# A two-block transformer layer on one core: second half of two gate products by tile, rotary key in other PSUM banks, first turned tiles under the side input's products

## The chip, the cores and the metric

The kernel runs on one core of one Trainium2 chip. The metric is device time in microseconds (us) from one launch to its end, the median over several runs. A profiled execution gives a trace of every instruction. The engines are TensorE (PE), VectorE (DVE), ScalarE (ACT), GpSimd (POOL) and SyncE (SP). Work that PE does is written to PSUM, which has eight banks of 128 partitions by 512 floats.

## The reference

The reference takes 512 tokens of width 1024 through four mixers. The last two are the layers of `second_block`. Each of these ends in a gated side input, and this is what the change touches:

```python
for i in range(DEPTH):
    xn = rmsnorm_2(x, norm_g[i])
    if i % N_MIXERS == 0:
        y = mixer_na(xn, na_w_in[j], na_rpb[j], na_w_out[j])
    else:
        y = mixer_mla(xn, mla_w_in[j], mla_q_norm[j], mla_w_qb[j],
                      mla_kv_norm[j], mla_w_kvb[j], mla_w_out[j])
    h = x + y
    gate = jax.nn.sigmoid(rmsnorm_2(h, ple_norm[i]) @ ple_w_gate[i])
    x = h + gate * (p[i] @ ple_w_proj[i])
return rmsnorm_2(x, final_norm)
```

`mixer_mla` begins with `xn @ w_in`, whose columns are c_q (384), c_kv (256), the rotary key (32) and z (1024). The rotary key is multiplied with cosines and sines.

## The kernel before

Every product in float32 is made of three: high part by low part, low by high, high by high. A weight matrix comes in units of 1 MB (128 x 2048 floats). SP loads a unit into `w_raw` (L308), ACT writes its rounded high part `w_hi` (L339, `split_high`), POOL writes the rest `w_lo` (L348, `split_low`) and counts up `w_ready`. There are three slots of such units. SP loads unit n once PE has signalled that the unit before it in the slot is used up (`consumed`): `w_used` for the first unit of a pair, `bank_done` for the second.

Activations are four tiles of 128 tokens. To be multiplied, a tile of x is squared and summed on ACT (`square_x`, L658), POOL makes the reciprocal root (`root_x`, L704 and L706), DVE scales it (`norm_tile`, L746), PE transposes it with 8 transposes into two of the banks 4 to 7 (`turn_tile`, L623), ACT copies it to `u_hi` (`high_tile`, L664) and DVE writes the rest to `u_lo` (`low_tile`, L752). Each step waits for the one before it by a semaphore (`chain_x_square`, `chain_x_rstd`, `chain_normed`, `chain_turned`, `chain_high`, `chain_low`).

The order on each engine is written out by hand in one function for each engine and stage. The stages that matter, in order, twice (layer 0 with `na_out` and `ple0`, layer 1 with `mla_out` and `ple1`):

- `na_out` or `mla_out`, a product of 1024 to 1024 in two halves of 512 columns (i = 0, 1). Each half has two weight units (a = 0, 1) and four tiles (j), with all tiles of unit a = 0 before those of a = 1. DVE adds it to x (L591).
- `ple_tensor`: the side input's product, two halves of four tiles of 6 matmuls each. Between them PE turns the four tiles of the normalised residual.
- `gate_tensor`: the gate's product, again two halves with two units each, which are called g0, g1 (i = 0) and g2, g3 (i = 1) below. One (a, j) is 12 matmuls. ACT takes a finished bank through the sigmoid (`take`, L1778), DVE multiplies it with the side input (L1815) and adds it to x (L1818).
- In layer 0, `mla_cq` (units cq0, cq1, 384 columns) and `mla_ckv` (ckv0, ckv1, 256 columns) follow, then `mla_rope` (one unit, 48 matmuls of 512 columns) and `mla_z`. In `mla_cq` PE turns the rest of the next chain's tiles: `project_turning` takes rows of (a, j, tile to turn in the middle). Layer 1 ends with the last norm and the store of the output by SP (L328).

The first entries in the list that sets where tiles are turned in `mla_cq` and the function that takes the rotary key read:

```python
INTERLEAVED = ((0, 0, 1), (0, 1, 2), (1, 0, 3), (0, 2, None), ...
project_tensor(pe, "mla_rope", banks=2)          # banks 0 and 1
project_tensor(pe, "mla_z", only=(0,))           # banks 0 to 3
```

`wait_bank` lets PE write a bank when both takers' counts (`bank_free`) have passed it, so `mla_z` in bank 0 waits for DVE's product with the cosines (L1942).

Of the kernel before, what the change touches and what calls it, by code (L numbers as in the profile page):

```python
# [24 lines left out]
NT = T // P  # L25
# [74 lines left out]
def _program(nc, A, out):  # L100
    with ExitStack() as ctx:
# [523 lines left out]
                tr.then_inc(chain_turned, 1)  # L625

        HALF_BY_HALF = ((0, 0, 2), (0, 1, 3), (0, 2, None), (0, 3, None), (1, 0, None), (1, 1, None), (1, 2, None), (1, 3, None))
        INTERLEAVED = ((0, 0, 1), (0, 1, 2), (1, 0, 3), (0, 2, None), (0, 3, None), (1, 1, None), (1, 2, None), (1, 3, None))

        def project_turning(pe, c, name, order):  # L630

            run = RUNS[name]
            for a, j, turning in order:
                pe.wait_ge(w_ready, run["unit"] + a + 1)
                if a == 0:
                    wait_bank(pe, run, 0, j)
                    pe.wait_ge(chain_low, c.two + 2 * (j + 1))
                mm = products(pe, run, 0, a, j, between=None if turning is None else lambda: turn_tile(pe, c, turning))
                if a == 0 and j == 3:
                    mm.then_inc(w_used, 1)  # L640
                if a == 1:
                    mm.then_inc(bank_done, 1)

        def square_y(act, c, name, i, j):
            act.wait_ge(bank_done, 4 * (RUNS[name]["block"] + i) + j + 1)
# [1030 lines left out]
        def ple_tensor(pe, c, nth):  # L1676

            run = RUNS[f"ple{nth}_proj"]
            pe.wait_ge(p_lo, nth + 1)
            turning = {(0, 0): 1, (0, 2): 2, (1, 0): 3}  # L1680
            for i in range(2):
                pe.wait_ge(w_ready, run["unit"] + 1)
                for j in range(NT):
                    wait_bank(pe, run, i, j)
                    products(pe, run, i, 0, j).then_inc(bank_done, 1)
                    if (i, j) in turning:
                        turn_tile(pe, c, turning[i, j])
# [77 lines left out]
        def gate_tensor(pe, c, name, chain):  # L1765
            pe.wait_ge(chain_low, c.two + 2 * NT)
            project_tensor(pe, name, only=(0,))
            project_tensor(pe, name, only=(1,), between=chain and {(1, 1, 3): lambda: turn_tile(pe, chain, 0)})

        def gate_scalar(act, c, nth):  # L1770

            name = f"ple{nth}_gate"
            run = RUNS[name]

            def take(i, j):
                act.wait_ge(bank_done, 4 * (run["block"] + i) + j + 1)
                act.wait_ge(e_used, 8 * nth + 4 * i + j + 1)
                nc.scalar.activation(at(SIG + j * 512), bank(j), ACT.Sigmoid).then_inc(bank_free["act"], 1)  # L1778

            split_next(act, name, 0, 0)  # L1780
            for j in range(NT):
                take(0, j)
            split_next(act, name, 0, 1)
            if c is final_chain:
                take(1, 0)
                take(1, 1)
                square_x(act, c, 0)
                take(1, 2)
                square_x(act, c, 1)
                take(1, 3)  # L1790
                square_x(act, c, 2)
                square_x(act, c, 3)
                return
            split_next(act, name, 1, 0)
            take(1, 0)
            take(1, 1)
            square_x(act, c, 0)
            take(1, 2)
            square_x(act, c, 1)
            high_tile(act, c, 0)  # L1800
            take(1, 3)
            split_next(act, name, 1, 1)
            square_x(act, c, 2)
            high_tile(act, c, 1)
            square_x(act, c, 3)
            high_tile(act, c, 2)
            high_tile(act, c, 3)

        def gate_vector(dve, c, nth):
# [11 lines left out]
                take(0, j)  # L1821
            wait_gain(dve, c.pre)
            take(1, 0)
            take(1, 1)
            norm_tile(dve, c, 0)
            take(1, 2)
            if c is final_chain:
                norm_tile(dve, c, 1)
                take(1, 3)
                norm_tile(dve, c, 2)  # L1830
                norm_tile(dve, c, 3)
                return
            low_tile(dve, c, 0)
            norm_tile(dve, c, 1)
            take(1, 3)
            low_tile(dve, c, 1)
            norm_tile(dve, c, 2)
            norm_tile(dve, c, 3)
            low_tile(dve, c, 2)
            low_tile(dve, c, 3)  # L1840

        def gate_pool(pool, c, nth):

            n = RUNS[f"ple{nth}_gate"]["unit"] + 2
            split_low(pool, n)
            split_low(pool, n + 1)
            if c is final_chain:
                for t in range(NT):
                    root_x(pool, c, t)
                return  # L1850
            for part in range(4):
                split_low(pool, n + 2, part)
            root_x(pool, c, 0)
            root_x(pool, c, 1)
            split_low(pool, n + 3, 0)
            split_low(pool, n + 3, 1)
            root_x(pool, c, 2)
            root_x(pool, c, 3)
            split_low(pool, n + 3, 2)
            split_low(pool, n + 3, 3)  # L1860


        COS, SIN = gain[0][:, 0:T], gain[0][:, T:2 * T]
# [71 lines left out]

        def mla_rope_vector(dve):

            dve.wait_ge(rope_in, 16)

            def take(i, j):  # L1940
                if j == 0:
                    return nc.vector.tensor_tensor(at(ROPE_TMP), bank(0), COS, ALU.mult)  # L1942
                return nc.vector.tensor_tensor(at(QT), bank(1), SIN, ALU.mult)
            project_vector(dve, "mla_rope", take, banks=2)
            run = RUNS["mla_rope"]
            dve.wait_ge(bank_free["dve"], 4 + run["taken"] + 4)
            done("dve", nc.vector.tensor_tensor(at(QT), at(QT), at(ROPE_TMP), ALU.add))
            settle("dve", dve)
            nc.vector.tensor_scalar(k_rope[0], at(QT), 1.0, None, ALU.mult).then_inc(rope_high, 1)
# [51 lines left out]
        def _(pe):  # L2001
# [28 lines left out]
            for name in ("na_z", "na_q"):  # L2030
# [3 lines left out]
            begin(pe, na_flow)  # L2034
            pair_tensor(pe, na_flow)
            project_tensor(pe, "na_out", gated_by=na_flow, only=(0,), begun=True)
            project_tensor(pe, "na_out", gated_by=na_flow, only=(1,),
                           between={(1, 1, 3): lambda: turn_tile(pe, ple_chains[0], 0)})
            ple_tensor(pe, ple_chains[0], 0)
            gate_tensor(pe, ple_chains[0], "ple0_gate", mla_chain)  # L2040
            project_turning(pe, mla_chain, "mla_cq", INTERLEAVED)
            project_tensor(pe, "mla_ckv")
            project_tensor(pe, "mla_rope", banks=2)
            project_tensor(pe, "mla_z", only=(0,))
            project_tensor(pe, "mla_z", only=(1,), between={(1, 1, j): (lambda j: lambda: latent_turn(pe, j))(j) for j in range(NT)})
            pe.wait_ge(lat_low, 2 * NT)
            for name in ("mla_k", "mla_v", "mla_q"):
# [4 lines left out]
            project_tensor(pe, "mla_out", gated_by=mla_flow, only=(1,),  # L2052
                           between={(1, 1, 3): lambda: turn_tile(pe, ple_chains[1], 0)})
            ple_tensor(pe, ple_chains[1], 1)
            gate_tensor(pe, ple_chains[1], "ple1_gate", None)

# [314 lines left out]
```

## Time and profile before

| | us |
|---|---|
| median of 3 runs | 1464.06 (1461.59 to 1464.49) |
| profiled execution | 1463.27 |
| its span in the trace | 1461.5 |
| PE busy | 1373.1 (94%) |
| ACT, DVE, POOL busy | 716.3, 621.6, 780.9 |
| granted PE clock, mean | 0.985 |

The profiled execution took 1.8 us more than its span: what lies around the trace. PE is busy for most of the span, so that time can be found where PE waits. The gate of layer 0 stands in the trace at about 1036 to 1080 us, `mla_cq` to `mla_rope` at 1081 to 1130, the gate of layer 1 at 1408 to 1451, and the last norm behind it.

### The profile page before, as it was taken

The numbers are of one execution on the slowest core, as the hardware profiler recorded it, in microseconds if no ns is written. First come the engines' busy times: TensorE is split into PE (matmuls) and PEld (weight loads), VectorE is DVE, ScalarE is ACT, GpSimd is POOL, SyncE is SP. The second block draws the span as 40 slices with busy tenths as digits, with TensorE's granted clock in tenths as the row PEclk, the third lists the DMA queues.
The fourth block names the chain that finished last, engine by engine and source line by source line (L and its number), as shares of the span: only waits on it lengthen the run. The fifth ranks groups of instructions, "written<-read, shape, count | busy, mean of one in ns | idle before, by whom it ended". The sixth has DMA issues, their size and how long they took to land.

```text
span 1461.5 us, 20933 instructions
## 1 busy us (share of the span) xinstructions
PE 1373.1 (94%) x7818; PEld 1125.8 (77%) x7818; DVE 621.6 (43%) x1606; ACT 716.3 (49%) x1533; POOL 780.9 (53%) x729
## 2 busy tenths in 40 slices
PE   6999999998989999998999999889999999999997
PEld 5887877777878888776778887678878886778785
DVE  3322178886250011883420013962341145887144
ACT  4244278886342323773423234963443354787252
POOL 5355266666554534474753353886456334566652
PEclk9999999999999999889999999999999999999999
DMA  6233210000443231212343233324225221001521
GB/s 238 88 116 115 92 56 27 31 30 32 156 141 119 87 116 58 73 44 91 140 129 131 87 110 118 120 89 161 101 93 196 98 87 59 1 1 59 187 87 58
DMA packets 27876, 139.57 MB, mean 95 GB/s; under 512 B 3328, under 2 KB 3712, under 8 KB 16128
## 3 DMA queue, kind: packets, MB, share of 16 engines
q1 hardware_dynamic: 14112, 98.57, 18.7%
q10 hardware_dynamic: 13664, 39.66, 7.9%
q8 instruction: 63, 1.03, 0.3%
q14 instruction: 37, 0.30, 0.1%
HBM read 129.83 MB, written 8.39 MB: 95 GB/s over the span
## 4 chain that ended last, share of the span: by engine, by line
PE 71%; POOL 11%; DVE 9%; ACT 5%; issue 2%; DMA 1%; ACTq 0%; POOLq 0%; SPq 0%; DVEq 0%
PE psum L393 57%; POOL w_lo L348 3%; POOL w_free L1342 3%; PE psum L1183 3%; PE psum L1164 2%; PE psum L1136 2%; DVE w_free L1232 2%; PE psum L877 2%; DVE u_lo L1245 2%; POOL split L1359 1%; ACT w_hi L339 1%; DVE arena L746 1%; ACT u_hi L1285 1%; PE psum L1149 1%; POOL split L1355 1%
## 5 line engine op out<-in xcount | busy, mean ns | idle before, releaser
L348 POOL TENSOR_TENSOR w_lo<-w_raw,w_hi 128x2048 fp32r<-128x2048 f32 (+2 forms) x118 | 427.0, 3632 | 431.8 <-ACT w_hi L339 431.0
L393 PE MATMUL psum<-u_lo,w_hi 128*128 128x512 f32 (+1 forms) x712 | 279.8, 393 | 0.9 <-DVE arena L1942 0.9
L393 PE MATMUL psum<-u_hi,w_lo 128*128 128x512 f32 (+1 forms) x712 | 277.3, 389 | 0.0
L393 PE MATMUL psum<-u_hi,w_hi 128*128 128x512 f32 (+1 forms) x712 | 277.3, 389 | 0.0
L339 ACT ACTIVATE w_hi<-w_raw 128x2048 fp32r<-128x2048 f32 (+1 forms) x93 | 172.9, 1859 | 155.0 <-DMA w_raw<-in_weights 101.8
L393 PE MATMUL psum<-w_hi,split 128*128 128x512 f32 x608 | 195.7, 394 | 6.0 <-POOL w_lo L348 4.3
L794 ACT ACTIVATE w_free<-w_free,neg_max 128x256 f32<-128x256 f32 (+3 forms) x320 | 183.6, 580 | 12.5 <-DVE neg_max L916 7.4
L393 PEld LDWEIGHTS psum<-u_lo,w_hi 128*128 128x128 f32 (+1 forms) x712 | 133.2, 187 | 30.3 <-POOL w_lo L348 1.3
L393 PEld LDWEIGHTS psum<-u_hi,w_hi 128*128 128x128 f32 (+1 forms) x712 | 133.2, 187 | 28.8
L393 PEld LDWEIGHTS psum<-u_hi,w_lo 128*128 128x128 f32 (+1 forms) x712 | 133.2, 187 | 27.3
L393 PE MATMUL psum<-w_hi,u_lo 128*128 128x512 f32 (+2 forms) x352 | 135.8, 386 | 10.0 <-DVE u_lo L752 7.6
L1245 DVE TENSOR_TENSOR u_lo<-psum,u_hi 128x512 fp32r<-128x512 f32 (+3 forms) x256 | 124.5, 519 | 35.3 <-ACT u_hi L1285 32.3
L393 PEld LDWEIGHTS psum<-w_hi,split 128*128 128x128 f32 x608 | 114.2, 188 | 32.0 <-POOL w_lo L348 6.3
L1285 ACT ACTIVATE u_hi<-psum 128x512 fp32r<-128x512 f32 (+3 forms) x256 | 108.8, 463 | 51.9 <-PE psum L1164 48.1
L393 PE MATMUL psum<-w_hi,u_hi 128*128 128x512 f32 (+2 forms) x352 | 133.4, 379 | 0.0
L393 PE MATMUL psum<-w_lo,u_hi 128*128 128x512 f32 (+2 forms) x352 | 133.3, 379 | 0.0
L1164 PE MATMUL psum<-ident,w_free 128*128 128x128 f32 x704 | 110.6, 283 | 23.4 <-POOL w_free L1342 16.9
L393 PE MATMUL psum<-w_lo,split 128*128 128x512 f32 x304 | 118.4, 390 | 0.0
L1164 PEld LDWEIGHTS psum<-ident,w_free 128*128 128x128 f32 x704 | 77.1, 141 | 48.8 <-POOL w_free L1342 27.8
L1342 POOL TENSOR_SCALAR w_free<-w_free,inv 128x256 f32<-128x256 f32 (+1 forms) x128 | 73.6, 590 | 65.5 <-DVE inv L1238 65.3
L1183 PE MATMUL psum<-u_lo,split 128*128 128x256 f32 (+1 forms) x416 | 102.9, 284 | 0.0
L510 DVE SCALAR_TENSOR_TENSOR split<-psum,split 128x512 fp32r<-128x512 f32 x40 | 27.6, 692 | 171.2 <-ACT split L502 157.2
(193 smaller groups left out, 2194.0 us busy)
## 6 DMA issues: line engine op xcount, KB each, us to landing
w_raw<-in_weights SPq DMA_DIRECT2D x90, 1024.0 KB, 4.8
x<-x_scratch ACTq DMA_DIRECT2D x12, 512.0 KB, 6.7
gain<-in_gains ACTq DMA_DIRECT2D x10, 512.0 KB, 4.6
gain<-in_strips ACTq DMA_DIRECT2D x16, 256.0 KB, 2.9
spare<-in_strips ACTq DMA_DIRECT2D x16, 256.0 KB, 2.9
x_scratch<-x ACTq DMA_DIRECT2D x16, 256.0 KB, 4.2
gain<-in_near ACTq DMA_DIRECT2D x8, 512.0 KB, 4.5
w_raw<-in_near ACTq DMA_DIRECT2D x8, 512.0 KB, 3.7
```

The costliest lines, as they stand in the source:

```text
L339: high = nc.scalar.activation(w_hi[b][:, c], w_raw[b][:, c], ACT.Copy)
L348: low = nc.gpsimd.tensor_tensor(w_lo[b][:, c], w_raw[b][:, c], w_hi[b][:, c].bitcast(F32), ALU.subtract)
L393: mm = nc.tensor.matmul(dst, lhs, rhs, start=(a == 0 and k == 0 and (wl, ul) == (0, 1)), stop=(a + 1 == u and k + 1 == nk and (wl, ul) == ...
L794: nc.scalar.activation(p_map(f, i, m, n), p_map(f, i, m, n), ACT.Exp, scale=-1.0, bias=stat_of(neg_max, i, m), accum_out=stat_of(row_sum, ...
L877: mm = nc.tensor.matmul(head_bank(d, r), buf[:, pt:pt + P], split[:, a + v:a + v + P], start=(kt == 0 and nth == 0), stop=(kt == kts[-1] a ...
L1136: mm = nc.tensor.matmul(score_place(f, i, m), *products[m][nth], start=(nth == 0), stop=(nth == 2 and f is not mla_flow))
L1164: tr = nc.tensor.transpose(psum[:, 4 + m, kt * P:(kt + 1) * P], p_map(f, i, m, n)[:, kt * P:(kt + 1) * P], ident[:])
L1183: mm = nc.tensor.matmul(dst, value_place(f, d, m, kt), pt_pair(buf, d, m, a, b), start=(br == 0 and m == 0 and kt == order[0] and nth == 0 ...
L1232: nc.vector.tensor_tensor_reduce(out=p_map(f, i, m, n), in0=score_bank(i, m, n), in1=bias_of(f, i, m), scale=-1.0, scalar=BIG, op0=ALU.add ...
L1245: nc.vector.tensor_tensor(u_lo[:, c], bank(4 + m, n), u_hi[:, c].bitcast(F32), ALU.subtract).then_inc(f.low, 1)
L1285: nc.scalar.activation(u_hi[:, pt_cols(i, m, n)], bank(4 + m, n), ACT.Copy).then_inc(f.high, 1)
L1342: nc.gpsimd.tensor_scalar(p_map(f, i, m, n), p_map(f, i, m, n), stat_of(inv, i, m), factor_of(f, i, m), ALU.mult, ALU.mult).then_inc(f.p, 1)
```

## The change

There are four edits, and no arithmetic changes.

1. The second half of both gates goes through a new function `project_by_tile`: for each tile both units (a = 0, then 1), so that one tile is complete before the next begins. In layer 0, tiles 0 and 1 of the next chain are turned in the middle of (a, j) = (0, 2) and (0, 3) of it. Before, all four tiles of a = 0 came first, and tile 0 was turned in the middle of (1, 3).
2. ACT, DVE and POOL follow in that order: each take of a tile is followed by that tile's square, root and norm. ACT splits g3 behind the first take of the first half rather than behind the fourth. POOL splits cq0 in two pairs of quarters, each behind a wait for a norm, and cq1 whole behind the last root.
3. `mla_cq` uses `TWO_TO_TURN`: tiles 2 and 3 are turned in the middle of (0, 0) and (0, 2), and all of a = 0 stands before a = 1. The rotary key's product goes to banks 4 and 5, and DVE counts its four banks as free ahead of time.
4. In both layers tile 0 of the chain for the gate is turned behind the first tile of the side input's product, not in the middle of the last tile of `na_out`/`mla_out`; tiles 1, 2, 3 are turned behind (0, 1), (0, 3) and (1, 1), not (0, 0), (0, 2) and (1, 0).

```diff
+        TWO_TO_TURN = ((0, 0, 2), (0, 1, None), (0, 2, 3), (0, 3, None), (1, 0, None), (1, 1, None), (1, 2, None), (1, 3, None))
...
+        def project_by_tile(pe, name, gated_by, between):
+
+            run = RUNS[name]
+            for j in range(NT):
+                for a in range(2):
+                    pe.wait_ge(w_ready, run["unit"] + 2 + a + 1)
+                    if a == 0:
+                        wait_bank(pe, run, 1, j)
+                    mm = products(pe, run, 1, a, j, gated_by=gated_by, between=between.get((a, j)))
+                    if a == 0 and j == 3:
+                        mm.then_inc(w_used, 1)
+                mm.then_inc(bank_done, 1)
...
-            turning = {(0, 0): 1, (0, 2): 2, (1, 0): 3}
+            turning = {(0, 0): 0, (0, 1): 1, (0, 3): 2, (1, 1): 3}
...
-            project_tensor(pe, name, only=(1,), between=chain and {(1, 1, 3): lambda: turn_tile(pe, chain, 0)})
+            project_by_tile(pe, name, None, {(0, 2): lambda: turn_tile(pe, chain, 0), (0, 3): lambda: turn_tile(pe, chain, 1)} if chain else {})
...
             if c is final_chain:
-                take(1, 0)
-                take(1, 1)
                 square_x(act, c, 0)
-                take(1, 2)
-                square_x(act, c, 1)
-                take(1, 3)
-                square_x(act, c, 2)
-                square_x(act, c, 3)
+                for j in range(1, NT):
+                    take(1, j)
+                    square_x(act, c, j)
                 return
...
             take(1, 0)
-            take(1, 1)
             norm_tile(dve, c, 0)
...
+            for j in range(1, NT):
+                take(1, j)
+                if c is not final_chain:
+                    low_tile(dve, c, j - 1)
+                norm_tile(dve, c, j)
+            if c is not final_chain:
+                low_tile(dve, c, 3)
...
         def mla_rope_vector(dve):
 
+            dve.wait_ge(bank_free["dve"], 4 + RUNS["mla_rope"]["taken"])
+            dve.sem_inc(bank_free["dve"], 4)
             dve.wait_ge(rope_in, 16)
...
+            dve.wait_ge(bank_done, 4 * RUNS["mla_rope"]["block"] + 4)
+            done("dve", nc.vector.tensor_tensor(at(ROPE_TMP), bank(4), COS, ALU.mult))
+            done("dve", nc.vector.tensor_tensor(at(QT), bank(5), SIN, ALU.mult))
+            settle("dve", dve)
...
-            project_tensor(pe, "na_out", gated_by=na_flow, only=(1,),
-                           between={(1, 1, 3): lambda: turn_tile(pe, ple_chains[0], 0)})
+            project_tensor(pe, "na_out", gated_by=na_flow, only=(1,))
...
-            project_turning(pe, mla_chain, "mla_cq", INTERLEAVED)
+            project_turning(pe, mla_chain, "mla_cq", TWO_TO_TURN)
             project_tensor(pe, "mla_ckv")
-            project_tensor(pe, "mla_rope", banks=2)
+            project_tensor(pe, "mla_rope", banks=2, base=4)
```

The order of instructions shows this at three places. The first is PE in the second half of layer 0's gate (L393 is a product, L623 the transposes of one tile; slot 0 holds g2, slot 1 holds g3, slot 2 holds cq0). Before, around the turning of tile 0:

```order
L393 MATMUL psum<-w_hi1_52,u_hi_49 128x512
L623 MATMUL psum<-ident,arena_65 128x128 x8
L393 MATMUL psum<-w_hi1_52,u_lo 128x512
L393 MATMUL psum<-w_lo1_55,u_hi_49 128x512
L393 MATMUL psum<-w_hi1_52,u_hi_49 128x512
L393 MATMUL psum<-w_hi1_52,u_lo 128x512
L393 MATMUL psum<-w_lo1_55,u_hi_49 128x512
L393 MATMUL psum<-w_hi1_52,u_hi_49 128x512
L393 MATMUL psum<-w_hi2_53,u_lo 128x384
```

In the changed kernel, around the turning of the same tile, the rows on PE are:

```order
L393 MATMUL psum<-w_hi1_52,u_hi_49 128x512
L393 MATMUL psum<-w_hi0_51,u_lo 128x512
L393 MATMUL psum<-w_lo0_54,u_hi_49 128x512
L393 MATMUL psum<-w_hi0_51,u_hi_49 128x512
L393 MATMUL psum<-w_hi0_51,u_lo 128x512
L393 MATMUL psum<-w_lo0_54,u_hi_49 128x512
L393 MATMUL psum<-w_hi0_51,u_hi_49 128x512
L623 MATMUL psum<-ident,arena_65 128x128 x8
L393 MATMUL psum<-w_hi0_51,u_lo 128x512
```

Tile 0 was turned six products before the gate's end, in g3's last tile; now it is turned in tile 2 of g2, behind a product with g3 that belongs to tile 1.

The second place is ACT in the second half of the same gate (L339 splits a unit, L1778 or L1792 is a take, L658 or L672 a square, L664 or L678 the high copy of a turned tile). Before:

```order
L1778 ACTIVATE arena_65<-psum 128x512 x4
L339 ACTIVATE w_hi1_52<-w_raw1_58 128x2048
L339 ACTIVATE w_hi2_53<-w_raw2_59 128x2048
L1778 ACTIVATE arena_65<-psum 128x512 x2
L658 ACTIVATE arena_65,stat<-x 128x1024
L1778 ACTIVATE arena_65<-psum 128x512
L658 ACTIVATE arena_65,stat<-x 128x1024
L664 ACTIVATE u_hi_49<-psum 128x4x128 x2
L1778 ACTIVATE arena_65<-psum 128x512
L339 ACTIVATE w_hi0_51<-w_raw0_57 128x2048
L658 ACTIVATE arena_65,stat<-x 128x1024
```

The changed kernel has on ACT, from the same first take on:

```order
L1792 ACTIVATE arena_65<-psum 128x512
L339 ACTIVATE w_hi1_52<-w_raw1_58 128x2048
L1792 ACTIVATE arena_65<-psum 128x512 x4
L339 ACTIVATE w_hi2_53<-w_raw2_59 128x2048
L672 ACTIVATE arena_65,stat<-x 128x1024
L1792 ACTIVATE arena_65<-psum 128x512
L678 ACTIVATE u_hi_49<-psum 128x4x128 x2
L672 ACTIVATE arena_65,stat<-x 128x1024
L1792 ACTIVATE arena_65<-psum 128x512
L678 ACTIVATE u_hi_49<-psum 128x4x128 x2
L672 ACTIVATE arena_65,stat<-x 128x1024
```

The split of g3 (slot 1) moved ahead of three takes, and the first square now follows the first take of the second half; the split of cq1 (slot 0) moved behind the last square.

The third place is POOL in the same gate (L348 writes a low part, L704/L706 or L718/L720 are a root). Before:

```order
L348 TENSOR_TENSOR w_lo2_56<-w_raw2_59,w_hi2_53 128x512 x4
L704 TENSOR_SCALAR stat<-stat 128x1
L706 TENSOR_TENSOR stat<-stat,half_exp 128x1
L704 TENSOR_SCALAR stat<-stat 128x1
L706 TENSOR_TENSOR stat<-stat,half_exp 128x1
L348 TENSOR_TENSOR w_lo0_54<-w_raw0_57,w_hi0_51 128x512 x2
```

The changed kernel has on POOL, from behind g3's split to cq1's:

```order
L718 TENSOR_SCALAR stat<-stat 128x1
L720 TENSOR_TENSOR stat<-stat,half_exp 128x1
L348 TENSOR_TENSOR w_lo2_56<-w_raw2_59,w_hi2_53 128x512 x2
L718 TENSOR_SCALAR stat<-stat 128x1
L720 TENSOR_TENSOR stat<-stat,half_exp 128x1
L348 TENSOR_TENSOR w_lo2_56<-w_raw2_59,w_hi2_53 128x512 x2
L718 TENSOR_SCALAR stat<-stat 128x1
L720 TENSOR_TENSOR stat<-stat,half_exp 128x1
L718 TENSOR_SCALAR stat<-stat 128x1
L720 TENSOR_TENSOR stat<-stat,half_exp 128x1
L348 TENSOR_TENSOR w_lo0_54<-w_raw0_57,w_hi0_51 128x2048
```

The low part of cq0 was written ahead of all roots and now comes in two pairs of quarters between them; that of cq1 was interleaved with the last roots and now stands whole behind them.

## Rows read from the trace of the kernel before

**Rows 1.** Page, part 1: busy time of each engine
```profile
PE 1373.1 (94%) x7818; PEld 1125.8 (77%) x7818; DVE 621.6 (43%) x1606; ACT 716.3 (49%) x1533; POOL 780.9 (53%) x729
```
**Rows 2.** Timeline of PE, gate's end to `mla_z`: start, length, line, [idle before, releaser]
```profile
1080.96 0.42 PE L393 MATMUL psum<-w_hi,u_lo 128*128 128x384 f32 x1 [0.28 <-DVE u_lo L752]
...
1082.09 1.07 PE L623 MATMUL psum<-ident,arena 128*128 128x128 f32 x8
1082.92 0.42 PE L393 MATMUL psum<-w_hi,u_lo 128*128 128x384 f32 x1
...
1086.11 0.41 PE L393 MATMUL psum<-w_hi,u_lo 128*128 128x384 f32 x1 [1.88 <-DVE u_lo L752]
...
1088.04 1.97 PE L623 MATMUL psum<-ident,arena 128*128 128x128 f32 x8
...
1092.20 0.44 PE L393 MATMUL psum<-w_hi,u_lo 128*128 128x384 f32 x1 [1.05 <-POOL w_lo L348]
...
1130.42 0.47 PE L393 MATMUL psum<-u_lo,w_hi 128*128 128x512 f32 x1 [0.95 <-DVE arena L1942]
```
**Rows 3.** Windows: stretch, length, busy of five engines, granted PE clock, DMA share, GB/s
```profile
1087.00:1088.00 1.00, 0.91 (x3) 0.40 (x2) 0.98 (x1) 0.00 (x0) 1.00 (x1) 0.50 0.05 16
1098.00:1100.00 2.00, 2.00 (x14) 2.00 (x13) 0.00 (x0) 1.36 (x1) 0.00 (x0) 1.00 1.04 412
```
**Rows 4.** Chain that ended last, in order of time: start, length, what
```profile
738.52 156.51 PE psum L393 x690
...
1094.38 5.23 PE psum L393 x30
1099.63 6.24 DMA w_raw<-in_weights
1105.89 1.92 ACT w_hi L339
1107.88 4.62 POOL w_lo L348
1112.54 16.94 PE psum L393 x96
```
**Rows 5.** Timeline of ACT, POOL and DVE in layer 0's gate
```profile
1049.58 0.60 ACT L1778 ACTIVATE arena<-psum 128x512 f32<-128x512 f32 x1 [3.29 <-PE psum L393]
1050.93 0.69 DVE L1818 TENSOR_TENSOR x<-x,arena 128x512 f32<-128x512 f32 x1
...
1074.55 1.05 ACT L658 ACTIVATE arena<-x 128x1024 f32<-128x1024 f32 x1
1076.26 0.57 POOL L706 TENSOR_TENSOR stat<-stat,half_exp 128x1 f32<-128x1 f32 x1
1076.87 1.28 DVE L746 SCALAR_TENSOR_TENSOR arena<-x,stat,gain 128x1024 f32<-128x1024 f32 x1 [0.76 <-POOL stat L706]
```
**Rows 6.** Page, part 6: issues of weight units, KB, median us to landing
```profile
w_raw<-in_weights SPq DMA_DIRECT2D x90, 1024.0 KB, 4.8
```
**Rows 7.** Timeline of POOL, DVE and PE at the side input's product, layer 0
```profile
1024.98 4.61 POOL L348 TENSOR_TENSOR w_lo<-w_raw,w_hi 128x2048 fp32r<-128x2048 f32 x1
1027.10 3.57 DVE L746 SCALAR_TENSOR_TENSOR arena<-x,stat,gain 128x1024 f32<-128x1024 f32 x1
1030.73 1.09 PE L623 MATMUL psum<-ident,arena 128*128 128x128 f32 x8 [0.91 <-DVE arena L746]
1032.05 1.29 DVE L752 TENSOR_TENSOR u_lo<-psum,u_hi 128x512 fp32r<-128x512 f32 x2 [0.18 <-ACT u_hi L664]
```
**Rows 8.** Timeline of ACT and DVE behind the last gate
```profile
1451.59 0.60 ACT L1778 ACTIVATE arena<-psum 128x512 f32<-128x512 f32 x1 [1.08 <-PE psum L393]
1452.03 1.28 DVE L746 SCALAR_TENSOR_TENSOR arena<-x,stat,gain 128x1024 f32<-128x1024 f32 x1 [0.45 <-POOL stat L706]
1453.95 0.69 DVE L1818 TENSOR_TENSOR x<-x,arena 128x512 f32<-128x512 f32 x1
1457.14 1.28 DVE L746 SCALAR_TENSOR_TENSOR arena<-x,stat,gain 128x1024 f32<-128x1024 f32 x1 [0.75 <-POOL stat L706]
```

More of the change, by code:

```diff
@@ L1780, in gate_scalar @@
             split_next(act, name, 0, 0)
-            for j in range(NT):
+            take(0, 0)
+            split_next(act, name, 0, 1)
+            for j in range(1, NT):
                 take(0, j)
-            split_next(act, name, 0, 1)
+            take(1, 0)
             if c is final_chain:
-                take(1, 0)
-                take(1, 1)
                 square_x(act, c, 0)
-                take(1, 2)
-                square_x(act, c, 1)
-                take(1, 3)
-                square_x(act, c, 2)
-                square_x(act, c, 3)
+                for j in range(1, NT):
+                    take(1, j)
+                    square_x(act, c, j)
                 return
             split_next(act, name, 1, 0)
-            take(1, 0)
+            square_x(act, c, 0)
             take(1, 1)
-            square_x(act, c, 0)
+            high_tile(act, c, 0)
+            square_x(act, c, 1)
             take(1, 2)
-            square_x(act, c, 1)
-            high_tile(act, c, 0)
+            high_tile(act, c, 1)
+            square_x(act, c, 2)
             take(1, 3)
+            high_tile(act, c, 2)
+            square_x(act, c, 3)
             split_next(act, name, 1, 1)
[L1803 to L1806, printed above, removed]
             high_tile(act, c, 3)
@@ L1823, in gate_vector @@
             take(1, 0)
-            take(1, 1)
             norm_tile(dve, c, 0)
[L1826 to L1840, printed above, removed]
+            for j in range(1, NT):
+                take(1, j)
[4 more added lines that the diff above has]
+                low_tile(dve, c, 3)
         def gate_pool(pool, c, nth):
@@ L1850, in gate_pool @@
                 return
-            for part in range(4):
-                split_low(pool, n + 2, part)
             root_x(pool, c, 0)
+            pool.wait_ge(chain_normed, c.n + 1)
+            split_low(pool, n + 2, 0)
+            split_low(pool, n + 2, 1)
             root_x(pool, c, 1)
-            split_low(pool, n + 3, 0)
-            split_low(pool, n + 3, 1)
+            pool.wait_ge(chain_normed, c.n + 2)
+            split_low(pool, n + 2, 2)
+            split_low(pool, n + 2, 3)
             root_x(pool, c, 2)
             root_x(pool, c, 3)
-            split_low(pool, n + 3, 2)
-            split_low(pool, n + 3, 3)
+            split_low(pool, n + 3)
         COS, SIN = gain[0][:, 0:T], gain[0][:, T:2 * T]
@@ L1936, in mla_rope_vector @@
         def mla_rope_vector(dve):
+            dve.wait_ge(bank_free["dve"], 4 + RUNS["mla_rope"]["taken"])
+            dve.sem_inc(bank_free["dve"], 4)
             dve.wait_ge(rope_in, 16)
[L1940 to L1946, printed above, removed]
+            dve.wait_ge(bank_done, 4 * RUNS["mla_rope"]["block"] + 4)
+            done("dve", nc.vector.tensor_tensor(at(ROPE_TMP), bank(4), COS, ALU.mult))
+            done("dve", nc.vector.tensor_tensor(at(QT), bank(5), SIN, ALU.mult))
+            settle("dve", dve)
             done("dve", nc.vector.tensor_tensor(at(QT), at(QT), at(ROPE_TMP), ALU.add))
@@ L2051, in _ @@
             project_tensor(pe, "mla_out", gated_by=mla_flow, only=(0,), begun=True)
-            project_tensor(pe, "mla_out", gated_by=mla_flow, only=(1,),
-                           between={(1, 1, 3): lambda: turn_tile(pe, ple_chains[1], 0)})
+            project_tensor(pe, "mla_out", gated_by=mla_flow, only=(1,))
             ple_tensor(pe, ple_chains[1], 1)
```

## The prediction

> **What bounds the kernel now.** I read the page's busy table first: PE works 94% of the span [rows 1], so only stops of PE, or the stretch behind its last product, can be gained. I then read PE's timeline in the stretches that the diff touches. In layer 0 the trouble lies between the gate's end and `mla_z`: stops of 0.28 and 1.88 us for a low half of a turned tile, 1.05 for cq1's low part, 0.95 for DVE's product with the cosines, and a turned tile that took 1.97 instead of 1.07 [rows 2]. In that stretch the granted clock was 0.50, the 1.2 GHz level [rows 3]; the 1.88 us stop stands just ahead of it. The chain of waits adds a stop for ckv1: its load took 6.24 us, ACT 1.92, POOL 4.62, and only then did PE go on at 1112.54 [rows 4]. At the side input's product one turned tile waits 0.91 us [rows 7]. Behind the last gate PE is done, and take, product, sum, square, root, norm and store of tile 3 remain in a row [rows 8].
>
> **How much there is.** Steps: 690 products of 512 columns in 156.51 us are 0.227 each; 30 of 384 columns in 5.23 are 0.173, if the drain of the last is left off [rows 4]. A row says 0.39 us or so for a product whose next may start 0.23 later, so an idle entry understates a stop by some 0.16. `mla_ckv`'s second half and `mla_rope` take 16.94 for 96 products [rows 4]; less 48 x 0.227 and the drain, a 256-column product is 0.12. A turned tile costs 0.83 to the next product [rows 2], about 0.9 with that one's slower start. From the moment PE wanted tile 0 (1077.9: 7.5 groups of 12, at 2.72, behind the second half's start at 1057.5, for which see below) to `mla_z` at 1130.42 [rows 2] are 52.5 us. The work in it is 6 x 0.227 + 4 x 0.9 + 96 x 0.173 + 96 x 0.12 + 48 x 0.227 = 44.0 us. So 8.5 us there are stops and slow clock, and no edit can gain more at this place.
>
> **Gate of layer 0, by tile.** The work is the same; a group of 12 products is 2.72 us. The first take starts at 1049.58 [rows 5], 0.2 behind its bank, so the second half starts at 1057.5. Now a tile is complete every 5.44 us: 1063.0, 1068.4, then with one turned tile each 1074.8 and 1081.1. PE wants tile 0 at 1069.8 and tile 1 at 1076.1.
> What must be ready: from a take's start to x's sum are 2.04 us (1049.58 to 1051.62) [rows 5]; from the square's start to the norm's end 3.6 (1074.55 to 1078.15) [rows 5]. Tile 0: take 1063.2, sum 1065.2, ACT splits cq0 until 1065.6, square, norm done at 1069.1. That is 0.7 us ahead of PE.
> Tile 1 meets the lock. On rows, DVE's norm started at 1027.10 and took 3.57 us instead of 1.28, until 1.1 us after POOL's split of 4.61 us had ended [rows 7]: with both inputs in SBUF, DVE stands still until POOL's instruction is through. Here POOL's quarters (1.2 each, a quarter of 4.6) are released by norm 0, at the same time as the take of tile 1: DVE's two instructions wait for one or two quarters. Sum at 1072.8, square behind the high copy of tile 0, norm at 1076.3: PE stops 0.2 us. In the same way tile 2: take 1075.0, sum 1078.8, norm 2 at 1082.3.
> The Trainium skill's page "SBUF — State Buffer", section "Who interferes with whom", says that a DVE instruction with two SBUF inputs and a GpSimd one that reads SBUF exclude each other for a whole instruction, and that whoever comes first wins. By that rule the 0.2 stands; if the two only slowed one another a little it would be 0, and the sum 0.2 better. It matters more for a rival below.
> Moving g3 forward: PE now wants it 2.72 us into the second half, at 1060.2, not at 1068.4. Its slot is free after the first half's first four groups (1046.7); load 4.8 [rows 6], ACT 1.92, POOL 4.62 [rows 4] give 1058.1: 2 us to spare, and the same in layer 1. POOL's 4.6 us hold up DVE's sums of the first half until 1062.4, just ahead of tile 0's.
>
> **`mla_cq` in the new order.** PE comes at 1081.1 + 0.2. Six products of (0, 0), then tile 2 at 1082.4, when norm 2 is there. (0, 1) and half of (0, 2) end at 1087.5. Norm 3: DVE's sum 1083.6, ACT's high copy of tile 2 until 1084.2 (a turned tile's start to its low half's end is 2.6 us [rows 7], of which the low half is 0.7 behind the high one), square, norm at 1087.6: 0.2 us of stop. Its high copy stands behind the split of cq1 on ACT, low half at 1090.1 against 1089.6 wanted: 0.5. cq1's slot is now given back at 1078.6 instead of 8 us earlier, but its load is done by 1083.4 and waits for ACT (1087.1) and POOL (behind norm 3, until 1092.2); PE wants it at 1092.2: 0 to 0.1. The 48 products of a = 1 end at 1100.5; before, `mla_cq` ended 66 products behind the turned tile at about 1094.2 [rows 4], at 1105.6.
> Then the weight units. ckv0: ACT issues four stores of x and the rotary table first (some 4 us), splits at 1093.7, POOL ends at 1100.3: just in time. ckv1: its slot is free when a = 0 is through, at 1092.2; before, three groups and ckv0 (12 us) stood against 6.24 + 1.92 + 4.62 = 12.8 and the semaphores; now four groups and ckv0 (14.1 us) do. The load overlaps more of the stores: 2 MB, 0.5 MB and 1 MB at the 412 GB/s that this place has reached [rows 3] need 8.9 us from about 1091, so up to 1 us later. I take 0.2 of stop. The rotary unit: slot free at 1100.5, 4.8 + 1.92 + 4.62 and the semaphores are 11.5, PE's `mla_ckv` is 11.5: 0.1.
> Rotary key: banks 4 and 5 have been read by the low halves before, so `mla_z` starts in bank 0 at once; the 0.95 [rows 2] and its 0.16 go. DVE's work on the key then runs under 20 us of `mla_z`.
> Left over: 0.2 + 0 + 0.2 + 0.5 + 0.1 + 0.2 + 0.1 = 1.3. Gain 8.5 - 1.3 = 7.2. No stop is near 1.88 us, so I expect the clock at its high level. Behind `mla_z` all loads hang on PE's own progress, and what is won stays.
>
> **Side input's product, both layers.** POOL's whole split follows root 3 and blocks norm 3 [rows 7]. Tile 0 is now turned 1.36 x 2 us later; ACT's square 3 stands behind its high copy, so it comes 1.25 later, and root, split and norm 3 with it (end 1031.9 instead of 1030.67). But PE asks for tile 3 one group of 6 later too, 1.36 us: the stop stays at 0.9. The gate waits for the low half of tile 3; 2.72 us of products now hide it instead of 4.08, and from the tile's start at 1030.73 to its low half's end at 1033.34 were 2.6 us [rows 7], where PE now has 0.9 + 2.7 us of work: hidden, 1 us to spare. Term: 0, between -0.9 (the stop goes) and +1 (a place in ACT's queue slips) a layer.
>
> **The tail.** In layer 1 PE ends at the same distance. Before, take 3 was done at 1452.19, but DVE was in norm 1 until 1453.31 and ended the sum at 1454.64; last norm from 1457.14 [rows 8]. Now tile 2 is 5.44 us ahead, its norm done by 1451.7, and tile 3 has the engines alone: sum at 1453.6 (2.04 behind 1451.59), norm's start at about 1455.8, as root 3 no longer stands behind norm 2 either. Term: -1.3, between -0.9 and -1.5.
>
> **Sum.** 7.2 + 0 + 1.3 = 8.5. The profiled execution took 1463.27, 0.8 less than the median of the runs; 1463.3 - 8.5 = 1454.8, and on the median's scale 1464.06 - 8.5 = 1455.6.
>
> **Rivals.**
> - *A (0.49)*: as above, 1455.6, its own range 1454 to 1457.5.
> - *B (0.15), the weight units bound `mla_cq` to `mla_rope`.* For: three of them come within 0.3 us of the time wanted, and loads share the queues with the stores [rows 3]. Against: each is released by PE's earlier progress. A load at 8.5 us instead of 6.24, and ckv0 a little late, cost 2 to 3: 1458.3.
> - *C (0.12), norms late under the gate.* A take, high copy or quarter misses its place, turned tile 1 or 2 waits over 1.88 us, and the clock drops as it did in rows 3 (about 1.8 us: 0.9 in the turned tile and as much in six or seven products). Cost 3 to 4: 1459.3.
> - *D (0.08), side input.* Tile 0 later holds square 3 and the take of the side input's banks more than I think: 1 us in each layer, 1457.7.
> - *E (0.06), the gain is swallowed ahead of the next attention,* since a load or x's stores set `mla_z`'s pace. Only the tail stays: 1462.7. Against: `mla_z` ran without a stop.
> - *F (0.04), norm 3 behind cq1's split.* The split is whole now, and if POOL gets it first, DVE's norm 3 is 4.6 us late, as at [rows 7], with a slow clock behind it: 1461.5. Against: root 3 is 0.9 us behind the square, the split at least 1.9. It is the case in which that rule of the Trainium skill's page "SBUF — State Buffer" would decide by who comes first.
> - *G (0.06), slower.* g3 is wanted 8 us earlier in both gates. If its load, ACT and POOL need over 6.2 us more than my 11.4, each gate stops by more than 4.2 us and all of the gain is gone; at 7.5 us more the time is 1466.5. For: the load stands in front of three takes on ACT. Against: a load of 6.24 is the worst that I saw, 1.4 over the usual.
>
> **The numbers.** Measurement of this kernel can tell 0.2%, 2.9 us: faster is below 1461.1. A to D are faster (0.84), E and F within (0.10), G slower (0.06). The range: the low end is A with nearly no left-over and the tail at its best, 1453.3; the high end takes in B, C and D, 1460.3. Outside lie E, F, G and 2 or 3 in 100 below.
>
> **What would show it.** In the changed profile: PE's first product of `mla_z` 7 us earlier, near 1123; between the gate and it no stop over 0.6 and the clock at 1.00; no stop for g3; turned tiles 0 and 1 within the gate with at most 0.2 ahead; tile 3 of the side input still waiting 0.9; no wait for L1945 in PE's rows; last norm 4.2 us behind the last take rather than 5.6. I am wrong if ckv1 or the rotary unit waits for DMA, or if a turned tile stops PE for 2 us.

## The result, and the profile after

The changed kernel took 1452.64 us (median of 4 runs, 1452.15 to 1453.58) against 1462.82 for the kernel before (4 runs): a ratio of 0.9932, 95% interval 0.9917 to 0.9947. Two more series gave 1453.20 (5 runs, ratio 0.9923, 0.9910 to 0.9937) and 1452.71 (4 runs, ratio 0.9921, 0.9901 to 0.9942). So the change brings 10 to 11 us. I had forecast 1455.6 and a gain of 8.5, with a range that ended at 1453.3. Sign and mechanism were right, the size was too small.

The profiled execution took 1453.12 us. The busy table of its page, to be read beside [rows 1]:

```profile
span 1451.3 us, 20932 instructions
...
PE 1368.2 (94%) x7818; PEld 1122.2 (77%) x7818; DVE 632.3 (44%) x1606; ACT 716.0 (49%) x1533; POOL 776.1 (53%) x726
```

PE's number of products is the same, but its busy time fell by 4.9 us: products at half clock count double, so a part of the gain is clock. DVE's rose by 10.7 without an instruction more: it stood at the lock with POOL, which its records count as busy.

PE's timeline from the gate to `mla_z`, the counterpart of [rows 2] (tiles 0 and 1 are turned at 1069.74 and 1076.08, tiles 2 and 3 at 1082.11 and 1087.18, all without a stop):

```profile
1089.94 0.41 PE L393 MATMUL psum<-w_hi,u_lo 128*128 128x384 f32 x1 [0.62 <-DVE u_lo L766]
...
1106.53 0.39 PE L393 MATMUL psum<-w_hi,u_lo 128*128 128x256 f32 x1 [0.20 <-POOL w_lo L348]
...
1123.30 0.39 PE L393 MATMUL psum<-u_lo,w_hi 128*128 128x512 f32 x1
```

Only the 0.62 and the 0.20 are left of five stops (four in [rows 2] and ckv1's 0.96 ahead of the product at 1112.54 in [rows 4]), and `mla_z` starts at 1123.30 without one, 7.1 us earlier than in [rows 2]. Windows of the same trace show the clock where it was at 0.50 in [rows 3]:

```profile
1085.00:1088.00 3.00, 3.00 (x21) 2.82 (x20) 1.28 (x1) 1.80 (x2) 1.97 (x3) 1.00 0.14 55
```

The chain of waits, to be read beside [rows 4], shows what the 0.20 is: the load of ckv1 takes 7.54 us now, but PE's work over it has grown too.

```profile
1089.94 2.33 PE psum L393 x12
...
1092.29 7.54 DMA w_raw<-in_weights
...
1099.86 1.93 ACT w_hi L339
...
1101.85 4.63 POOL w_lo L348
...
1106.53 23.50 PE psum L393 x125
```

Behind the last gate, beside [rows 8]:

```profile
1442.79 0.60 ACT L1792 ACTIVATE arena<-psum 128x512 f32<-128x512 f32 x1 [2.21 <-PE psum L393]
1443.42 0.69 DVE L1826 TENSOR_TENSOR arena<-arena 128x512 f32<-128x512 f32 x1 [0.56 <-ACT arena L1792]
...
1446.99 1.28 DVE L760 SCALAR_TENSOR_TENSOR arena<-x,stat,gain 128x1024 f32<-128x1024 f32 x1 [2.16 <-POOL stat L720]
```

DVE is idle when take 3 ends, and from the last take's start to the last norm's start are 4.20 us instead of 5.55.

By the two traces the 10.15 us of span are: 7.1 from the gate's start to `mla_z`, 0.1 behind `mla_z`'s first product, 0.2 at the two side inputs together, 1.35 in the tail, and 1.5 in the last attention, which no edit touches; the changed kernel's trace was 0.1 behind ahead of all edits. The 1.5 lie in this window of the kernel before, where PE ran at half clock for 3.4 us:

```profile
1240.00:1244.00 4.00, 4.00 (x26) 2.57 (x26) 1.23 (x4) 1.04 (x5) 1.41 (x3) 0.57 0.00 0
```

The same work lies 7.25 us earlier in the changed kernel. This window holds most of it (it begins 0.75 us before that work):

```profile
1232.00:1236.00 4.00, 3.18 (x30) 1.84 (x26) 2.12 (x8) 2.52 (x8) 2.15 (x4) 1.00 0.02 4
```

### The profile page after: what moved, and what is told of

The parts are those of the page before. It is cut to its first block, busy times and chain, and to the rows that moved or that the text cites. A ratio compares the mean times of both kernels' runs of the same rounds, so it can differ in the third digit from the quotient of the medians.

```text
span 1451.3 us, 20932 instructions
## 1 busy us (share of the span) xinstructions
PE 1368.2 (94%) x7818; PEld 1122.2 (77%) x7818; DVE 632.3 (44%) x1606; ACT 716.0 (49%) x1533; POOL 776.1 (53%) x726
## 4 chain that ended last, share of the span: by engine, by line
PE 72%; POOL 10%; DVE 9%; ACT 5%; issue 2%; DMA 1%; ACTq 1%; POOLq 0%; SPq 0%; DVEq 0%
PE psum L393 58%; POOL w_free L1356 3%; PE psum L1197 3%; PE psum L1178 2%; POOL w_lo L348 2%; PE psum L1150 2%; DVE w_free L1246 2%; DVE u_lo L1259 2%; PE psum L891 2%; POOL split L1373 1%; PE psum L1163 1%; ACT u_hi L1299 1%; ACT w_hi L339 1%; DMA w_raw<-in_weights 1%; DVE arena L760 1%
## 5 line engine op out<-in xcount | busy, mean ns | idle before, releaser
L348 POOL TENSOR_TENSOR w_lo<-w_raw,w_hi 128x2048 fp32r<-128x2048 f32 (+2 forms) x115 | 427.1, 3726 | 409.5 <-ACT w_hi L339 406.0
L393 PE MATMUL psum<-u_lo,w_hi 128*128 128x512 f32 (+1 forms) x712 | 279.7, 393 | 0.0
L393 PE MATMUL psum<-u_hi,w_lo 128*128 128x512 f32 (+1 forms) x712 | 277.3, 389 | 0.0
L393 PE MATMUL psum<-u_hi,w_hi 128*128 128x512 f32 (+1 forms) x712 | 277.3, 389 | 0.0
L339 ACT ACTIVATE w_hi<-w_raw 128x2048 fp32r<-128x2048 f32 (+1 forms) x93 | 172.9, 1859 | 158.4 <-DMA w_raw<-in_weights 105.0
L393 PE MATMUL psum<-w_hi,split 128*128 128x512 f32 x608 | 195.7, 394 | 6.1 <-POOL w_lo L348 4.4
L393 PEld LDWEIGHTS psum<-u_lo,w_hi 128*128 128x128 f32 (+1 forms) x712 | 133.2, 187 | 28.8 <-issue 0.2
L393 PEld LDWEIGHTS psum<-u_hi,w_hi 128*128 128x128 f32 (+1 forms) x712 | 133.1, 187 | 28.6
L393 PEld LDWEIGHTS psum<-u_hi,w_lo 128*128 128x128 f32 (+1 forms) x712 | 133.2, 187 | 27.7
L393 PE MATMUL psum<-w_hi,u_lo 128*128 128x512 f32 (+2 forms) x352 | 134.7, 383 | 8.3 <-DVE u_lo L766 7.7
L393 PEld LDWEIGHTS psum<-w_hi,split 128*128 128x128 f32 x608 | 114.2, 188 | 32.2 <-POOL w_lo L348 6.5
L393 PE MATMUL psum<-w_hi,u_hi 128*128 128x512 f32 (+2 forms) x352 | 133.1, 378 | 0.0
L393 PE MATMUL psum<-w_lo,u_hi 128*128 128x512 f32 (+2 forms) x352 | 132.9, 378 | 0.0
L393 PE MATMUL psum<-w_lo,split 128*128 128x512 f32 x304 | 118.4, 390 | 0.0
```

Source lines behind the costliest of these rows:

```text
L339: high = nc.scalar.activation(w_hi[b][:, c], w_raw[b][:, c], ACT.Copy)
L348: low = nc.gpsimd.tensor_tensor(w_lo[b][:, c], w_raw[b][:, c], w_hi[b][:, c].bitcast(F32), ALU.subtract)
L393: mm = nc.tensor.matmul(dst, lhs, rhs, start=(a == 0 and k == 0 and (wl, ul) == (0, 1)), stop=(a + 1 == u and k + 1 == nk and (wl, ul) == ...
```

## The experiments

The theory after the first result: each step gained what its stops in one trace had cost, and the rest came from how long those stops are in other executions, and from half clock that comes and goes. The rivals: an edit removed the stretch in the last attention, or the side input's part did more than I allowed.

**rope_only**, the rotary key's edit alone in the kernel before:

```diff
-            project_tensor(pe, "mla_rope", banks=2)
+            project_tensor(pe, "mla_rope", banks=2, base=4)
```

> The kernel before with one edit alone: the rotary key's product in banks 4 and 5. My theory: PE's stop of 0.95 us ahead of mla_z (1.1 by its steps) goes and stays gone, so -1.1 us and nothing else moves between the gate and mla_z. Rival (the stop is hidden anyway, or comes back at mla_z's weights): 0. For the 1.5 us more than forecast I hold that the stretch of half clock at the start of the last attention (1240 us in the trace of before) is not set by any edit; then this kernel, whose program is that of before up to there but for 1.1 us, may show it or not. Rival for the 1.5: an edit of the change removed it, then it is here as in before.

Measured 1461.54 against 1462.83, ratio 0.9995 (0.9984 to 1.0007), which cannot tell 1.1 us from 0. The trace can. From ckv1's stop to the middle of `mla_z` PE has no stop at all, and relative to the kernel before it gains 1.2 us there (50.8 us instead of 52.0). The 0.95 does not come back. In this trace PE ran the start of the last attention at full clock, although its instructions there are those of before.

**tail_only**, the final gate by tile alone:

```diff
+            if chain:
+                project_tensor(pe, name, only=(1,), between={(1, 1, 3): lambda: turn_tile(pe, chain, 0)})
+            else:
+                project_by_tile(pe, name, None, {})
```

> The kernel before with the final gate's second half by tile alone, with the takes, squares and norms in that order and g3 split behind the first take, in layer 1. My theory: -1.3 us, all behind PE's last product: last norm starts 4.2 us behind the last take instead of 5.6. Rival: the norms' order in the tail matters less, as the root and store of tile 3 set the end: -0.3. Ahead of the last gate the program is that of before to the instruction; a trace without the half clock at about 1240 us would show that this stretch comes and goes by itself, one with it would leave it open.

Measured 1461.69 against 1462.83, ratio 0.9993 (0.9983 to 1.0003). In its trace the last take starts at 1450.05 and the last norm at 1454.26: 4.21 us, the 1.3 of the sum. Again there was no half clock in the last attention. But there was a stretch at about 964 us, in the attention ahead of it, which the first trace of before has not.

**side_as_before**, the changed kernel without the side input's part:

```diff
-            turning = {(0, 0): 0, (0, 1): 1, (0, 3): 2, (1, 1): 3}
+            turning = {(0, 0): 1, (0, 2): 2, (1, 0): 3}
```

> The changed kernel with the side input's part undone: tiles turned where they were before, tile 0 in the last tile of the output product. My theory (term 0; 0.2 less of stop by the trace of after, per layer): +0.2 to +0.4 us against the changed kernel, so about -9.6 against before. Rival: the side input's part brought most of the 1.5 us that I had not forecast: +1.5 or more.

Measured 1453.42 (6 runs), ratio 0.9943 (0.9930 to 0.9957). That interval leaves room for the rival's 1.5 us; the trace does not. Tile 3's stop at the side input is back at 0.90 and 0.92 us, where it is 0.71 and 0.72 with the edit. The whole stretches ahead of the two gates are 0.6 us longer together than in the changed kernel's three traces (0.4 in that of no_rope_no_side, which lacks the edit too), not 1.5.

**quarters**, the changed kernel with one gate unit's low part (the one that POOL writes behind root 3) in four pieces at the side input:

```diff
-            split_low(pool, n + 3)
+            for part in range(4):
+                split_low(pool, n + 3, part)
```

> The changed kernel with one more edit: at the side input POOL writes the first gate unit's low part in four quarters, not whole. My theory (norm 3 stands still until POOL's instruction is through, for the whole of it): norm 3 starts after at most one quarter and takes 2 to 2.5 us at most instead of 3.57, ends 1.5 to 3 us earlier, and PE's stop of 0.7 us ahead of tile 3 goes in both layers: -1.4 to -1.8 us against the changed kernel. Rival (norm 3 is slow for another reason, or the low half is then the one that waits): 3.57 us stay, or the stop comes back behind it, 0.

Measured 1451.97 (6 runs), ratio 0.9930 (0.9918 to 0.9943): by the runs not to be told from the changed kernel, where I had expected 1.4 to 1.8 us less. The stop is gone in both layers, and from tile 0's turning to the gate are 13.1 us instead of 14.1. On DVE, norm 3 of the changed kernel and then of quarters read:

```profile
1028.42 3.57 DVE L760 SCALAR_TENSOR_TENSOR arena<-x,stat,gain 128x1024 f32<-128x1024 f32 x1
```

```profile
1026.38 1.48 DVE L760 SCALAR_TENSOR_TENSOR arena<-x,stat,gain 128x1024 f32<-128x1024 f32 x1
```

So the stop of 0.7 to 0.9 us was the lock with one whole POOL instruction, and a piece of a quarter lets DVE in between. The norm ended 1.08 us behind POOL's whole split in the changed kernel (1030.90) and 1.08 behind the second quarter here (1026.78); the third quarter, begun at 1026.74, then took 2.28 us instead of 1.28, as POOL now stood at the lock. By the trace the two layers gain 1.9 us together at this place, though that trace has 0.79 at ckv1's stop where the first trace of the changed kernel has 0.20.

**after_again**, the changed kernel once more:

> The changed kernel once more, for more runs and a second trace. By the stages of the two traces the change is worth 9.0 us (7.3 from the gate to the middle of mla_z, 1.35 in the tail, 0.4 at the side input); another 1.5 lies in a stretch of half clock at 1240 us that the one trace of before has and that of after has not. My theory: that stretch, and others in the attentions, come and go from one execution to the next, so over more runs the difference of the medians falls to 9 to 9.5 us. Rival (the change removed it for good): it stays at 10.2 or more, and the stretch is absent here too.

Measured 1453.20 against 1463.79: 10.6 us, not the 9 to 9.5 that I expected. The half clock in the last attention is absent again. So the chance of that stretch alone did not explain the size.

**late_g3**, the split of g3 behind the fourth take:

```diff
-            take(0, 0)
-            split_next(act, name, 0, 1)
-            for j in range(1, NT):
+            for j in range(NT):
                 take(0, j)
+            split_next(act, name, 0, 1)
```

> The changed kernel with ACT's split of g3 behind the fourth take of the first half, as before. My theory (by tile, g3 is wanted 2.7 us into the second half): its low part is then ready 4.5 us too late in both gates, so PE stops for 4 to 4.6 us twice, and half clock behind it may cost 1.7 each: +9 to +12 us against the changed kernel, about as slow as before. Rival (the chain of norms of cq has slack that takes the stop up, as PE waits there in any case): +4 to +5 in all, for the last gate alone.

Measured 1469.03 (10 runs), ratio 1.0025 (1.0014 to 1.0036): 15.8 us over the changed kernel's 1453.2 on the same chip, more than the 9 to 12 that I expected, and slower than before. The first row is PE's in layer 0's gate, the second in layer 1's:

```profile
1064.66 0.80 PE L393 MATMUL psum<-w_hi,u_lo 128*128 128x512 f32 x1 [4.34 <-POOL w_lo L348]
...
1437.24 0.80 PE L393 MATMUL psum<-w_hi,u_lo 128*128 128x512 f32 x1 [4.34 <-POOL w_lo L348]
```

The stops are the 4.5 us forecast (4.34 and the 0.16 that an idle entry hides), but the granted clock stayed at 0.50 behind each:

```profile
1064.00:1067.00 3.00, 2.34 (x6) 1.86 (x7) 0.00 (x0) 0.00 (x0) 0.61 (x1) 0.50 0.00 0
1067.00:1070.00 3.00, 3.00 (x9) 2.32 (x8) 0.00 (x0) 0.00 (x0) 0.00 (x0) 0.50 0.00 0
```

It was low for 6.8 us, twice as long as behind the 1.88 us stop of before. By the two traces each gate lost 7 to 7.3 us: 4.5 of stop and 2.5 to 2.8 of clock. The trace also had the half clock in the last attention, 1.5 us more. The slack of the rival does not exist. This move, three takes in ACT's queue, is the condition on which by tile pays at all.

**split_first**, cq1's split ahead of square 3 and root 3:

```diff
             high_tile(act, c, 2)
+            split_next(act, name, 1, 1)
             square_x(act, c, 3)
-            split_next(act, name, 1, 1)
...
-            root_x(pool, c, 3)
             split_low(pool, n + 3)
+            root_x(pool, c, 3)
```

> The changed kernel with cq1's high part ahead of square 3 on ACT and its whole low part ahead of root 3 on POOL. My theory (norm 3 sets when tile 3 is turned): norm 3 comes 5.4 us later, PE stops for some 5 us ahead of tile 3, the clock halves for a while as it did in the kernel before: +5.5 to +7.5 us. Rival (cq1's late low part is what holds mla_cq, norm 3 has slack): cq1 ready 4 us earlier, 0 or a gain.

Measured 1460.63 (10 runs), ratio 0.9981 (0.9969 to 0.9994): 7.4 us over the changed kernel. The forecast was 5.5 to 7.5. PE waits for norm 3 as forecast:

```profile
1090.93 0.47 PE L623 MATMUL psum<-ident,arena 128*128 128x128 f32 x1 [5.26 <-DVE arena L760]
```

The turned tile and what follows run at half clock (0.50 in the window 1091 to 1094). The place of whole splits behind the last root is right, though it makes cq1's low part later.

**no_rope_no_side**, the gates by tile and the new order of `mla_cq` only (the two diffs above, reversed and not):

> The changed kernel without the side input's part and without the rotary key's banks: both gates by tile, norms beneath, new order of mla_cq. My theory: PE's stop of 0.95 us behind mla_rope is back (1.1 by steps), 0.2 to 0.4 of the side input too: +1.3 to +1.5 us against the changed kernel, so by tile and the order carry 7.6 of the 9.0. Rival (the rotary key's edit gains nothing here, since the loads of mla_z or the key's work on DVE bind next): +0.3.

Measured 1454.28 (6 runs), ratio 0.9932 (0.9919 to 0.9945), 1.1 us over the changed kernel on that chip. In its trace the stop of 0.94 ahead of `mla_z` is back, and 1.2 us are lost there relative to the changed kernel. But ckv1's stop was 1.21 us here against 0.20, with no edit between the gate and it. That row pointed to the part still missing.

**before_b, before_c and after_b**, more traces of both kernels:

> The kernel before, for another trace. Measured so far: the medians differ by 10.2 and 10.6 us, the stages by 9.0. Theory one (chance): stretches of half clock in the unchanged stages come and go in both kernels, and this trace lacks some of those of the first. Theory two (the change lengthens or removes them): the stretch behind the 1.88 us stop at 1086 us, or the one at 1240, is here again and longer than 3.4 us.

> As the run ahead of it: one more trace of the kernel before. Theory one: the stretch at 1086 us is here, that at 1240 in some of the traces. Theory two: both in every trace of before and none in any of after.

> The changed kernel, for a third trace and more runs. Theory one: a stretch of half clock in the last attention may be here too. The time: 1453 us, 9 to 10.5 below before on the same chip.

The kernel before took 1465.85 and 1464.04 us in these two single runs, the changed one 1452.71 (median of 4). The chain of waits of before_b, beside [rows 4]:

```profile
1101.01 7.40 DMA w_raw<-in_weights
...
1108.44 1.92 ACT w_hi L339
...
1110.43 4.58 POOL w_lo L348
...
1115.05 18.43 PE psum L393 x96
```

The same load took 7.40 us instead of 6.24. PE stopped for 2.08 us and then ran at half clock, so that 96 products took 18.43 instead of 16.94: 2.6 us more than in the trace on which I built the sum. Over all my traces ckv1's stop was 0.96, 1.05, 1.46, 1.53 and 2.08 us with the old order, and none, 0.20, 0.57, 0.65, 0.68, 0.79, 0.88 and 1.21 with the new one (`mla_cq` in its new order, by tile, stores unmoved). I had happened on the shortest of the old order. The load itself took 6.24 to 7.40 us in the old order and 7.48 to 8.59 in these eight traces of the new one: it became slower, but PE had more work over it. The stretch in the last attention was in 2 of 5 traces of the old order (before and before_c), and with the new one in side_as_before, late_g3 and split_first, though not in the three of the changed kernel itself. So it comes and goes by itself, and theory one holds for that part. Neither theory had ckv1's stop, which varies from one execution to the next in both kernels and is shorter in the new order.

**stores_later**, quarters with ACT's stores of x behind the splits of ckv0 and ckv1:

```diff
+            project_scalar(act, "mla_cq")
             for t in range(NT):
                 act.dma_start(x_scratch[t * P:(t + 1) * P], x[:, t * D:(t + 1) * D]).then_inc(x_spilled, 16)
             load_rope(act)
-            project_scalar(act, "mla_cq")
```

> The kernel with quarters and one more edit: ACT issues x's four stores and the rotary table behind its splits of ckv0 and ckv1, not ahead of them. My theory (ckv1's load shares the DMA engines with 2 MB of stores, and its lateness is PE's stop of 0.2 to 1.2 us ahead of the second half of mla_ckv): the load lands in about 5 us instead of 6.2, the stop goes, -0.6 us against quarters on the average. Rival (the load is as slow without the stores, or ACT's late stores now hold mla_z, which overwrites x): 0 or slower.

Measured 1458.51 (5 runs) against 1463.62, ratio 0.9951 (0.9937 to 0.9965): 5.8 us slower than the changed kernel on that chip. I had expected 0.6 us less than quarters. ckv1's stop did go, as its load landed 5.1 us after its issue. But the stores then met the next load, that of the rotary unit, by the chain of waits:

```profile
1099.69 8.66 DMA w_raw<-in_weights
...
1110.37 4.53 POOL w_lo L348
...
1114.95 5.07 PE psum L393 x14
```

PE stopped for 3.78 us and ran at half clock for 3.4 us behind it. In both places the load that ran beside the stores was late; I had moved the lateness to a unit that PE has less work to cover.

## Why the prediction was off, point by point

- *"How much there is": 8.5 us, "and no edit can gain more at this place".* This is the step that failed. I took stops and clock of one execution as the kernel's own. The work in it (44.0 us) was counted right to 0.4 us; but in other traces of the old order ckv1's stop alone is up to 1.1 us longer, with half clock behind it once. By the three traces of the kernel before the place holds 8.5, 11.1 and 9.0 us, where I counted with the first. From the gate's first product to `mla_z`'s they took 94.6, 97.3 and 95.2 us, those of the changed kernel 87.6, 88.0 and 87.5. So the gain there, 7.2 in my sum, is 8.0 on the average.
- *Gate by tile.* Norms 0 and 1 were in time: no stop for either tile, 0.2 forecast for one (norm 1 ended at 1075.91, 0.4 earlier than forecast and 0.17 ahead of PE). The lock was as I had it: DVE's product in the first half took 4.71 us instead of 0.69, its sums were through at 1062.2 (1062.4 forecast), and nobody waited for them. g3 was in time, and late_g3 showed the price of the reverse.
- *`mla_cq` in the new order.* Tile 3's low half cost 0.62 (0.5 forecast), ckv1 0.20 (0.2 forecast), with a load of 7.54 where I allowed up to 7.2. `mla_z` at 1123.30; I had said near 1123. In this one trace the term of 7.2 was 7.1. That it fits is luck in part: the first trace of before had the shortest stop at ckv1 of its order, and that of after a short one too. The clock stayed at its high level from the gate to `mla_z` in all three traces of the changed kernel, as forecast.
- *Side input.* Term 0. The stop fell by 0.2 a layer, and the stretches ahead of the gates by 0.5 us together on the average of three traces each. Counted from the start of `na_out`, norm 3 ended 1.2 us later and PE asked for tile 3 1.4 us later. My text has 1.25 and 1.36, which already gives a shorter stop, not the same one.
- *Tail.* -1.3, measured -1.35, the same in tail_only.
- *The scale.* I put the gain on the median of three runs, 1464.06; with more runs the kernel before lies at 1462.8 to 1463.8. That moved the forecast up by 0.3 to 1.2 us. The result lies 0.7 us below the range; with 1462.8 as its base the range would have ended at 1452.1. So where the result fell against the range hung on three runs as much as on the terms, and the size of the gain, 10.2 to 10.9 against 8.5, is the firmer sign that a term was too small.
- *Rivals.* B (weights bound) and C (clock) did not decide. B's text says that loads and stores share queues; they are issued on two, SP's and ACT's, and what they share by [rows 3] is the 16 DMA engines. F's and G's mechanisms were real when forced; G's price was too low, as I had counted the stop and not the clock behind it: at a stop of 4.3 us in each gate I expected the loss of the whole gain, and measured more.
- *The range.* Below 1453.3 I had left only A at its best. There was no case in which the kernel before loses more, on the average, than its one trace shows.

Three traces of each kernel, stage by stage, give most of what was missing. The edits bring 8.0 us from the gate to `mla_z` (7.2 forecast), 0.1 behind `mla_z`'s first product (0), 0.5 at the two side inputs (0) and 1.35 in the tail (1.3): 10.0 us against 8.5. The medians differ by 10.2 to 10.9. What the other 0.2 to 0.9 us are is not settled. Stages that no edit touches differ by more than that between single traces, as half clock comes and goes there, and the median of the kernel before moved by 1.0 from one series to another.

## What to carry to other kernels

When products of a stage are reordered so that one tile is complete early, the norm, root and transpose chain of that tile can run under the products of the next; the price is that the second weight unit is wanted at once and the first one is given back late, so list both times for every unit. A stop is not a constant: before it goes into a sum as the most that can be gained, look at it in a second trace, above all where a load with neighbours on the DMA engines ends it. Count the clock behind a stop as well: here a stop that doubled cost more than double.

## What the hardware showed that I had not expected

- A stop of PE of 1.88 to 1.90 us was followed by 3.4 us at half clock in all five traces of the old order, and so was one of 2.40 to 2.42 at 723 to 727 us in all fourteen traces, that of 2.08 in before_b and that of 3.78 in stores_later. Stops of 1.47 to 1.57 (in other stages, before and after) were followed by none; those of 4.34 and 5.26 by 6.8 us. In the attentions, with stops under 1.5 us, a stretch of 3.4 us came in some executions and not in others, and cost 1.5 us.
- A load of 1 MB takes 4.8 us as a rule, 5.1 here with the stores out of its way, and 6.2 to 8.7 with 2 MB of stores beside it.
- DVE's instruction of 0.69 us took 4.71 behind a whole split on POOL; with the split in quarters, a norm of 1.28 took 1.48 and POOL's four quarters 6.01 instead of 4.61. Both lose a little, and the norm ends some 2 us earlier behind the split's start.
